# Attention of an encoder block spread over its projections, with row-paired scores and column-paired outputs

## The reference, cut to what matters

```
u = rmsnorm(h) ; [qA,kA,vA,qB,kB,vB] = u @ W_in            # 1024 x 2304, 18 blocks of 128 columns
oA: 8 query heads, 2 key/value heads, 64 wide; a chunk of 64 queries reads its own and the previous chunk,
    T5 bias, a sink per head in the softmax's maximum and sum
oB: 4 heads, two score maps each (64 wide), values 128 wide; chunk-causal; a = softmax(s0) - lam * softmax(s1)
    o = rmsnorm(a @ v, subln_g)
h = h + concat(oA, oB) @ W_out                              # 8 blocks
h = h + relu(rmsnorm(h) @ W_up)^2 @ W_down                  # 64 blocks
h = h + sigmoid(rmsnorm(h) @ W_gate) * (p @ W_ple) ; y = rmsnorm(h)
```

## Time and profile before

| | us |
|---|---|
| median of 3 runs | 1383.09 (1382.09 to 1386.27) |
| span of the profiled execution | 1379.7 |
| TensorE busy in it | 1333.9 (97%) |
| VectorE, ScalarE, GpSimd busy | 442.2, 355.9, 477.8 |
| granted TensorE clock, mean | 0.994 |

### The profile page before, as it was taken

How to read it: one execution, slowest core, us unless ns; L and a number is a source line. 1 busy time by engine, 2 the same in 40 slices (tenths; PEclk the granted TensorE clock), 3 DMA queues, 4 the chain that set the end, 5 groups by cost and what they waited for, 6 DMA issues and landing times.

```text
span 1379.7 us, 17463 instructions
## 1 busy us (share of the span) xinstructions
PE 1333.9 (97%) x6285; PEld 1090.7 (79%) x6285; DVE 442.2 (32%) x598; ACT 355.9 (26%) x655; POOL 477.8 (35%) x293
## 2 busy tenths in 40 slices
PE   6999999998888899999999999999999999999997
PEld 5788888995555788888888888888888888888886
DVE  5510112887888232222111221122211122222324
ACT  7112101665666311121011110011100122113221
POOL 3121231112221377433223432234322334774743
PEclk9999999999999999999999999999999999999999
DMA  5433111001000312111111121111121111113203
GB/s 190 173 94 92 46 46 31 0 1 31 1 0 0 138 46 60 32 59 47 46 46 46 47 60 46 46 46 46 46 60 46 46 46 46 48 43 98 70 0 123
DMA packets 117872, 75.38 MB, mean 55 GB/s; under 512 B 12817, under 2 KB 115250, under 8 KB 117458
## 3 DMA queue, kind: packets, MB, share of 16 engines
q1 hardware_dynamic: 117554, 73.93, 17.3%
q10 hardware_dynamic: 288, 1.05, 0.2%
HBM read 64.22 MB, written 10.75 MB: 54 GB/s over the span
## 4 chain that ended last, share of the span: by engine, by line
PE 90%; DVE 3%; ACT 2%; issue 2%; DMA 0%; DVEq 0%; SPq 0%; ACTq 0%
PE ps L787 77%; PE ps L812 3%; PE ps L903 2%; PE ps L928 2%; PE ps L970 2%; ACT e_buf L627 1%; PE ps L990 1%; PE ps L980 1%; PE ps L916 1%; DVE e_buf L1373 1%; PE ps L871 1%; DMA x_raw<-in_x 0%; PE ps L820 0%; PE ps L1072 0%; DVE coef L1368 0%
## 5 line engine op out<-in xcount | busy, mean ns | idle before, releaser
L366 POOL TENSOR_TENSOR w_lo<-w_raw,w_hi 128x1024 fp32r<-128x1024 f32 x96 | 230.9, 2406 | 621.7 <-ACT w_hi L551 621.6
L787 PE MATMUL ps<-u_hi,w_hi 128*128 128x512 f32 x896 | 277.0, 390 | 0.0
L787 PE MATMUL ps<-u_lo,w_hi 128*128 128x512 f32 x896 | 276.1, 389 | 0.0
L787 PE MATMUL ps<-u_hi,w_lo 128*128 128x512 f32 x896 | 275.8, 389 | 0.0
L551 ACT CAST w_hi<-w_raw 128x1024 fp32r<-128x1024 f32 x98 | 103.3, 1054 | 651.9 <-PE ps L787 651.1
L787 PEld LDWEIGHTS ps<-u_hi,w_lo 128*128 128x128 f32 x896 | 168.2, 188 | 35.1
L787 PEld LDWEIGHTS ps<-u_lo,w_hi 128*128 128x128 f32 x896 | 168.2, 188 | 35.1
L787 PEld LDWEIGHTS ps<-u_hi,w_hi 128*128 128x128 f32 x896 | 167.4, 188 | 35.7 <-issue 1.6
L787 PE MATMUL ps<-z_hi,w_hi 128*128 128x512 f32 x624 | 193.4, 391 | 0.0
L787 PE MATMUL ps<-z_hi,w_lo 128*128 128x512 f32 x624 | 192.1, 389 | 0.0
L787 PE MATMUL ps<-z_lo,w_hi 128*128 128x512 f32 x624 | 192.1, 389 | 0.0
(11 more groups left out here) (149 smaller groups left out, 1227.8 us busy)
## 6 DMA issues: line engine op xcount, KB each, us to landing
w_raw<-in_w_up SPq DMA_DIRECT2D x64, 256.0 KB, 3.0
w_raw<-in_w_down SPq DMA_DIRECT2D x64, 256.0 KB, 3.0
w_raw<-in_w_in SPq DMA_DIRECT2D x36, 256.0 KB, 3.2
x_raw<-in_x SPq DMA_DIRECT2D x8, 512.0 KB, 6.9
h_save<-h SPq DMA_DIRECT2D x1, 4096.0 KB, 11.1
w_raw<-in_w_out SPq DMA_DIRECT2D x16, 256.0 KB, 2.9
w_raw<-in_w_ple_gate SPq DMA_DIRECT2D x16, 256.0 KB, 3.0
out<-y_out SPq DMA_DIRECT2D x6, 512.0 KB, 5.1
```

Source lines behind the costliest of these rows:

```text
L366: nc.gpsimd.tensor_tensor(w_lo[:, s * D:(s + 1) * D], w_raw[:, s * D:(s + 1) * D], w_hi[:, s * D:(s + 1) * D].bitcast(F32), ALU.subtract). ...
L787: mm = nc.tensor.matmul(o[i], w, xx[:, x0[i]], start=(first and n == 0), stop=(last and n == 2))
```

## The change

The program of the five engines between the first two blocks and the MLP is written anew; before and after it only names and counts change.

- *Jobs.* Projections become jobs of one block and one token half, in banks 6 and 7 of PSUM in turn (`JOBS`); `project` can issue a job's 8 k-steps in pieces. Attention has banks 0 to 5. Value and output turns are jobs of 4 transposes.
- *B in the gaps.* k, q, v of head 0 and v of head 1 come first. In a head, a step (`step_b`) is: transposes of unit u, 2 k-steps (6 matmuls) of a projection, PV of u, 2 k-steps, scores of unit u+2, 2 k-steps. The 24 pieces of a head are the next head's k and q and the v after it; in the last two heads A's k, v and q of the first token half.
- *A in the gaps.* 16 slots of 4 heads, each with a piece after the transposes and one after PV: first A's queries of the second token half (32 k-steps over 12 pieces), then the output blocks of the first token half (64 k-steps over 20). The output blocks of the second half follow alone. A's q, k, v blocks and the output blocks are thus loaded and split once per token half, 14 blocks more; an output block's load is three transfers.
- *Row-paired scores.* q and k stay where the projection leaves them, 64 rows per map (B) or per key head (A); the two products use rows 0 to 63 and 64 to 127 and different banks. The `qs` copies go. A computes 192 of 256 keys (the first 64 of a tile are outside every query's window, and their exponentials are set to 0).
- *Transposed PV of A.* The values are stationary (64 columns), the transposed exponentials moving (256 columns: two heads); the output of a key head lands in 64 partitions, already transposed. GpSimd divides the exponentials by their sum before the transposes (`normalize`). The rows of the output weights are loaded in the matching order.
- *B's transposes* of a unit are made in one round into the bank of its scores, and copied at once; PV writes into the bank of its second map.
- The bias lines come one by one between the k-steps of the first query block.

```diff
+def in_head(hh):
+    if hh == 3:
+        return [("AQ0", 0, 6), ("AVT", 0, 6), ("AQ1", 0, 7), ("OT2", 0, 7), ("AQ2", 0, 6), ("OT2", 1, 6), ("AQ3", 0, 7),
+                ("AK", 1, 6), ("AV", 1, 7)]
+    k, q, vt, ot = f"K{hh + 1}", f"Q{hh + 1}", f"VT{hh + 1}", f"OT{hh - 1}"
+    jobs = [(k, 0, 6), (vt, 0, 6), (k, 1, 7), (vt, 1, 7), (q, 0, 6)]
+    jobs += [(ot, 0, 6)] if hh else []
+    jobs += [(q, 1, 7)]
+    jobs += [(ot, 1, 7)] if hh else []
+    return jobs + ([(f"V{hh + 2}", 0, 6), (f"V{hh + 2}", 1, 7)] if hh < 2 else [("AK", 0, 6), ("AV", 0, 7)])
+JOBS = [("Q0", 0, 6), ("Q0", 1, 7), ("VT0", 0, 6), ("VT0", 1, 7), ("V1", 0, 6), ("V1", 1, 7)]
+for _hh in range(B_HEADS):
+    JOBS += in_head(_hh)
+JOBS += [("AVT", 1, 7), ("AQ0", 1, 6), ("OT3", 0, 6), ("AQ1", 1, 7), ("OT3", 1, 7), ("AQ2", 1, 6), ("AQ3", 1, 7)]
+JOBS += [(f"O{j}", 0, 6 + j % 2) for j in range(DT)] + [(f"O{j}", 1, 6 + j % 2) for j in range(DT)]
...
+def a_share(q):
+    return range(-(-32 * q // 12), -(-32 * (q + 1) // 12))
+def o_share(q):
+    if q < 4:
+        return range(2 * q, 2 * q + 2)
+    return range(8 - (-7 * (q - 4) // 2), 8 - (-7 * (q - 3) // 2))
+def o_step(n):
+    if n < 16:
+        return n // 4 % 2, n % 4 + 4 * (n // 8)
+    return n // 8, n % 8
...
+            def load_out(j, r):
+                b = OUT0 + r * DT + j
+                cols = slice(j * P, (j + 1) * P)
+                sp.wait_ge(lo_done, b - 1)
+                sp.dma_start(raw(b % 2)[:, 4:8, :], wout_v[:, 4:8, cols]).then_inc(raw_full[b % 2], 16)
+                for g in range(2):
+                    sp.dma_start(raw(b % 2)[g * HD:(g + 1) * HD, 0:4, :], wout_a[:, 4 * g:4 * g + 4, cols]
+                                 ).then_inc(raw_full[b % 2], 16)
...
+            def normalize(v):
+                e3 = e_a[v % 2][:, :].rearrange("p (m k) -> p m k", k=256)[:, :, first_key(v):]
+                r = rden_a[:, 4 * (v % 2):4 * (v % 2) + 4].unsqueeze(2).to_broadcast([P, 4, 256 - first_key(v)])
+                pool.wait_ge(a_rd, v + 1)
+                nc.gpsimd.tensor_tensor(e3, e3, r, ALU.mult).then_inc(a_nr, 1)
...
+            def project(name, half, b, ns, ks=range(DT)):
+                for n in ns:
+                    if n == 0:
+                        pe.wait_ge(lo_done, b + 1)
+                        bank_for(name, half)
+                    mm = half_step(JOB_BANK[name, half], b % 2, half, ks[n], u_hi, u_lo, n == 0, n == DT - 1)
+                    if n == DT - 1:
+                        mm.then_inc(job_done, 1)
...
-            def score_b(hh, k, t):
-                u = TT * hh + k
-                n = (ORDER[k] + 1) * P
-                pe.wait_ge(qs_ok, AU + 2 * u + t + 1)
-                if isinstance(hh, int) and hh == 0 and k < 2:
-                    pe.wait_ge(a_e, 2 * TT - 1 + k)
-                    if k:
-                        pe.wait_ge(a_at, 2 * TT)
-                else:
-                    pe.wait_ge(a_e, AU + 2 * (u - 2) + t + 1)
-                for c in range(0, n, HALF):
-                    w = min(HALF, n - c)
-                    q0, s0 = (4 * t + k % 4) * P, s_at(k, t) + c
-                    mm = nc.tensor.matmul(ps[:, s0:s0 + w], qs[:, q0:q0 + P],
-                                          qkv[:, bass.ds((KB + hh) * T + c, w)], start=True, stop=True)
-                mm.then_inc(a_s, 1)
+            def score_b(u):
+                hh, k = u // TT, u % TT
+                n = keys_b(k)
+                if k == 0:
+                    for r in range(2):
+                        wait_taken(pe, f"Q{hh}", r)
+                if u >= 2:
+                    pe.wait_ge(b_oc, u - 1)
+                for c in range(0, n, HALF):
+                    w = min(HALF, n - c)
+                    for t in range(2):
+                        rows, s0 = slice(t * HD, (t + 1) * HD), s_at(k, t) + c
+                        mm = nc.tensor.matmul(ps[:, s0:s0 + w], q_b[hh % 2][rows, ORDER[k] * P:(ORDER[k] + 1) * P],
+                                              k_b[hh % 2][rows, c:c + w], start=True, stop=True)
+                        if c + w == n:
+                            mm.then_inc(b_s, 1)
...
-            def step_b(hh, k, ahead=True, prev=None):
-                h2, k2 = (hh, k + 2) if k < 6 else (hh + 1, k - 6)
-                if ahead:
-                    score_b(h2, k2, 0)
-                trans_b(hh, k, 0)
-                if prev is not None and k >= 3:
-                    pe.wait_ge(b_oc, TT * hh + k - 1)
-                    out_b(prev, k - 3)
-                if ahead:
-                    score_b(h2, k2, 1)
-                if ROUNDS[k] == 2:
-                    trans_b(hh, k, 1)
-                if prev is not None and k >= 3:
-                    pe.wait_ge(a_u_ok, TT + 2 * prev + k - 2)
-                if k or prev is not None:
-                    pv_b(*((hh, k - 1) if k else (prev, TT - 1)))
+                name, half, b = job_in(hh, p // 4)
+                project(name, half, b, range(2 * (p % 4), 2 * (p % 4) + 2))
+            def step_b(hh, k):
+                u = TT * hh + k
+                trans_b(u)
+                part_b(hh, 3 * k)
+                pv_b(u)
+                part_b(hh, 3 * k + 1)
+                if u + 2 < N_UNIT:
+                    score_b(u + 2)
+                else:
+                    score_a(u + 2 - N_UNIT)
+                part_b(hh, 3 * k + 2)
...
-                for j in range(4):
-                    mm = nc.tensor.matmul(ps[:, g * T + j * 256:g * T + (j + 1) * 256],
-                                          qs[:, (4 * g + j) * P:(4 * g + j + 1) * P],
-                                          qkv[:, bass.ds(KA * T + k0, 256)], start=True, stop=True)
-                mm.then_inc(a_s, 1)
+                for jj in range(2):
+                    for g in range(2):
+                        rows, c = slice(g * HD, (g + 1) * HD), s_a(v) + g * HALF + jj * 256
+                        mm = nc.tensor.matmul(ps[:, c + c0:c + 256], aq[2 * s + jj][rows, i * P:(i + 1) * P],
+                                              ak[rows, (i - 1) * P + c0:(i + 1) * P], start=True, stop=True)
+                mm.then_inc(a_s, 1)
...
-                for j in range(4):
-                    for kt in range(2):
-                        o, a = 6 * 512 + (4 * g + j) * HD, g * T + (2 * j + kt) * P
-                        mm = nc.tensor.matmul(ps[:, o:o + HD], at_buf[:, a:a + P],
-                                              qkv[:, bass.ds(VA * T + k0 + kt * P + g * HD, HD)],
-                                              start=(kt == 0), stop=(kt == 1))
-                mm.then_inc(a_o, 1)
+                for kt in range(kt0, 2):
+                    for g in range(2):
+                        c = (i - 1 + kt) * P + g * HD
+                        mm = nc.tensor.matmul(ps[g * HD:(g + 1) * HD, s_a(v):s_a(v) + 256], av[:, c:c + HD],
+                                              at_a[v % 2][:, kt * HALF + g * 256:kt * HALF + (g + 1) * 256],
+                                              start=(kt == kt0), stop=(kt == 1))
+                mm.then_inc(a_o, 1)
...
+            def part_a(q):
+                if q == 2:
+                    turn_av(1)
+                if q == 5:
+                    turn_o(3, 0)
+                if q == 8:
+                    turn_o(3, 1)
+                if q < 12:
+                    for n in a_share(q):
+                        project(f"AQ{n // DT}", 1, QA_BLOCK[1] + n // DT, [n % DT])
+                    return
+                for n in o_share(q - 12):
+                    j, step = o_step(n)
+                    if (j, step) == (0, 0):
+                        pe.wait_ge(sp_lo, 4)
+                    if (j, step) == (0, 4):
+                        pe.wait_ge(a_lo, 8)
+                    project(f"O{j}", 0, OUT0 + j, [step], BEHIND)
+            def step_a(v):
+                if v < N_SLOT - 2:
+                    score_a(v + 2)
+                trans_a(v)
+                part_a(2 * v)
+                pv_a(v)
+                part_a(2 * v + 1)
...
+            def step_b(hh, k):
+                u = TT * hh + k
+                if (hh, k) == (3, 0):
+                    early_hi(15)
+                if u < N_UNIT - 1:
+                    exp_b(u + 1, 0)
+                evac_b(u)
+                if u < N_UNIT - 1:
+                    exp_b(u + 1, 1)
+                take_b(u)
+                if u == N_UNIT - 1:
```

More of the change, by code:

```diff
@@ new lines, in build @@
+        x_raw = at("x_raw", [P, TT * D], F32, a_z + 32 * KB_)
+        lines = at("lines", [P, 12 * LINE], F32, a_z + 32 * KB_)
+        ak = at("ak", [P, T], F32, a_z)
+        av = at("av", [P, T], F32, a_z + 4 * KB_)
+        aq = [at(f"aq{j}", [P, T], F32, a_z + (8 + 4 * j) * KB_) for j in range(4)]
+        o_bt = [at(f"o_bt{hh}", [P, T], F32, a_z + (24 + 4 * hh) * KB_) for hh in range(B_HEADS)]
+        e_large = [at(f"e_large{t}", [P, T], F32, a_z + (40 + 4 * t) * KB_) for t in range(2)]
```

(68 more changed lines are left out.)

1194 lines of the change are left out of this document (621 added, 573 removed).

## The result

| | before | after |
|---|---|---|
| median of the runs | 1382.68 (1382.09 to 1386.27, 4 runs) | 1332.72 (1324.90 to 1342.36, 4 runs) |
| ratio, 95% interval | | 0.9639 (0.9586 to 0.9691) |
| profiled execution's span | 1379.7 | 1340.5 |
| first bias line, first matmul of the MLP | 48.57, 545.13 | 50.2, 505.9 |

The forecast was 1349 us in 1328 to 1380. The four runs are not one group: 1324.9 and 1325.1 us with a mean granted clock of 0.994 and 0.993, 1340.4 and 1342.4 with 0.979 and 0.978. No run lies near the median. The profiled execution is one of the second kind.

A forecast was written before the change was run, and what follows sets the result against it. TensorE, busy 97% of the span, was taken as the bound. 56.4 us less TensorE work, minus 22 us of waits, gave 34 us less: span 1345.7, plus 3.4 for the runs' median, 1349 us, range 1328 to 1380.

The forecast's parts named there:

- Row and column pairs: B's and A's scores and A's PV: paired matmuls overlap partly, taking 42.3, 12.5 and 16.4 us.
- five passes for eight: Paired scores: only one matmul's second pass runs beside the next one's first, so c pairs cost 2c+1 passes for 4c.
- the excursion: TensorE changing tiling mode and back: 0.4 us each, 75 of them, for bias lines, scores and A's PV.
- Rival 2: Better cover and overlap: waits go, 1327 us, or pairs overlap whole, 1332 us; chance 0.14.
- Waits: TensorE idle in attention: 14 us in B, 5 in A, 3 entering them; 22 us in all (0 to 46).
- its loop would cost half of what it cost before: B's loop through VectorE and ScalarE: half the earlier 1.7 us wait a pair, 14 us for 16 pairs.
- the 5 + 3 forecast: Waits around attention: 5 us for jitter in A's slots and 3 us for entering B and A.
- 12 x (0.648 + 0.4): The 12 single bias lines among projections: 12.5 us of TensorE, each with its own mode change.
- Rival 3: Slower: mode changes in B's scores and A's scores and PV cost 1.0 us each, giving 1394 us; chance 0.09.
- Rival 1: Pairs do not overlap: scores and PV grow by 37 us, 1367 to 1386 us, middle 1376; chance 0.12.
- The weights were hidden: Loads, casts and splits of 14 blocks stay covered by projections, the next ready 1.8 us early; no cost.
- near 511: Sign of being right: the first MLP matmul starts near 511 us.

The follow-up runs named there:

- e4: e1 with the score matmuls reordered so that fewer row pairs stand side by side, in B and A; 1320.06 us, ratio 0.9551.
- e5: e1 with A's PV doing both key tiles of one head group first, then of the other; 1320.26 us, ratio 0.9550.
- e8: e1 with all scores of B and A reading rows 0 to 63 only, so the output differs; 1357.98 us, ratio 0.9816.
- e1: The changed kernel with its bias lines in three groups of four, the first ahead of the wait for weights; 1320.66 us, ratio 0.9538.
- e6: e1 with B's three projection parts of each step in one lump behind the scores; 1381.00 us, ratio 0.9990.

## Why the prediction was right, point by point

The direction, the range and the mechanism held: fewer TensorE columns, and gaps filled with projections. The sizes did not all hold, and that the median lies only 16 us off is partly luck, since a low clock that the forecast did not have gave back a third of what it had too much. From 1349 to the 1332.7 of the runs lead three differences:

- **Row and column pairs: the step that failed.** I took "the value between that the order of passes gives", five passes for eight, on the ground that both passes of a matmul need the same rows and that the next pair waits its turn. The rows show whole overlap, 1.73 us for 1024 keys plus the excursion. That makes B's scores 31.1 for 42.3, A's scores 10.0 for 12.5 and A's PV 13.0 for 16.4: 17 us less. Both passes of one matmul do run one behind the other, but the other group does not stand still for it, and e4 and e5 showed that order is no ground at all. Of the page of the Trainium skill "TensorE: Matmul & The Clock Gate", Part 3, the near-simultaneous start gave the right value (some 4 ns on the page, 6 or 7 ns in this trace); strict program order, read across groups as I read it, would have cost e4 at least 0.86 us in each of B's 16 long units and did not. Rival 2 had this, at a chance of 0.14; it deserved more, since nothing but my reading of order spoke against it. That its 1332 is the median is luck: the runs are at 1325 and at 1341.
- **Waits.** Forecast 22 us, some 16 measured: the profiled comparison is 505.9 - 50.2 = 455.7 us, and 440.2 - 17.1 of work and 16.7 of low clock leave 15.9. Only 9.2 of them are waits by the view of waits (5.2 + 2.6 + 1.1 + 0.3); by my estimate some 4 more are the low clock at A's entry, 10 us at half speed of which 2 are idle, and the rest is not accounted for. B has 1 us a head in place of 3.5 (58.6 - 32.8 - 24.7); that its loop would cost half of what it cost before was a guess, and no run shows why it costs less. A and its entry had more than the 5 + 3 forecast, 7.8 of waits and those 4. I had searched that loop for what the slot's own work costs, and not for what the last head of B still leaves on GpSimd's queue.
- **The clock among the lines: a term missing.** I costed 12 single lines at 12 x (0.648 + 0.4) and nothing else. In half of the runs they cost 16.7 us more, about 8 in the median, which here lies between the two kinds. Nothing in the rows of before showed this: the clock was 1.00 among its grouped lines.

1349 - 17 - 6 + 8 = 1334.

What held: the excursion at 0.4 us also for 64 rows (2.13 - 1.73 and 0.82 - 0.43), and for 64 output partitions too (1.02 - 0.86 = 0.16 in the section, 2.29 - 9 x 0.228 = 0.24 behind it in e5). Rival 3, which needed 0.85, is out. Rival 1 is out by e8. A's slots at 7.94 us lie in the forecast 7 to 8.5. The weights were hidden except for one wait of 1.8 us. It stands ahead of the first line and so outside the comparison, which the forecast let begin there. The MLP starts at 505.94 for "near 511", but that is a hit by luck: this execution has the 16.7 us of low clock in it, and in e1, without them, the MLP starts at 484.67. The span from there on is 834.6 us for 834, so what follows the change is indeed the same:

```profile
505.94 0.61 PE L1009 MATMUL ps<-z_hi,w_hi 128*128 128x512 f32 x2
```

And the base of the whole sum, that gaps filled with projections hide the loop through VectorE and ScalarE, is shown by e6 from the other side: the same matmuls with unfilled gaps give 1381.

## What to carry to other kernels

Work that fills a gap is worth the wait that stood there and the clock that a wait takes with it; e6's waits were 47 us and its loss was 60. When work is moved into gaps, look at every small operation of the stage before that still stands in an in-order queue: one root of 1.6 us behind a split of 2.4 cost 6.5 us here. Look at all runs and their clocks before trusting a median: here it stood between two kinds of run. In this kernel, short and narrow matmuls in three groups between stretches of full ones never had the low kind, and one by one they had it in half of the runs.
